# First block's attention: the scores of twelve heads as two rounded products of stacked queries with split keys

## The chip, the core and the metric

The kernel is one program on one NeuronCore of a Trainium2 chip. The core has a matrix engine (TensorE, PE in the profile), a vector engine (VectorE, DVE), a scalar engine (ScalarE, ACT), a general engine (GpSimd, POOL), a queue of transfers (SyncE, SP), an on-chip memory (SBUF) and an accumulation memory of eight banks that PE writes (PSUM, `ps` in the profile). Each engine runs its own instructions in the order in which they were written down and waits for others on semaphores. The metric is the device time of one execution in microseconds (us), as a median over runs. A difference below about 0.3% can't be told from none.

## The reference, cut to what matters

Two transformer blocks run one after the other on 512 tokens. The first block has two layers, and in each of them 16 heads of 64 features attend in three ways. The change touches the products of queries and keys, `s` below, of heads 0 to 7 and of heads 12 to 15.

```python
# heads 0..7: a sliding window of 128 keys, two key heads (bnskd), four query heads on each
s = jnp.einsum('bnqkgd,bnskd->bnkgqs', qb, kb).astype(jnp.float32) * (HEAD_DIM ** -0.5)
...
p = jnp.exp(s - m)
# heads 8..11: blocks of 256 keys (left as they are)
s_own = (jnp.einsum('bhqd,bhsd->bhqs', qc, k_own).astype(jnp.float32) * scale + bias)
...
# heads 12..15: one key head for all, each query keeps its best 128 keys
score = jnp.einsum('bqhs,bqh->bqs', jax.nn.relu(dots), wi)
_, idx = lax.top_k(score, n_keep)
s = jnp.einsum('bqhd,bqkd->bhqk', qc, k_sel).astype(jnp.float32) * scale + bias
p = jax.nn.softmax(s, axis=-1).astype(v.dtype)
```

## The kernel before

Nearly all of the time is matrix products with weights. Each of these is made as three rounded products (`mm3`, lines 228 to 230, type fp32r, high by high, high by low and low by high), for which ACT rounds each weight tile (L192) and DVE subtracts to get what is left (L206). Between two such stages stands the attention of a layer, twice in the first block, from 497 to 597 us of the profile and again a thousand us later.

The attention of a layer is 64 units, numbered u = 16 * query block + head, each of 128 queries and one head, with 128 to 512 keys. Heads 0 to 7 (called A here) see 128 keys in the first query block and 256 in the others. Heads 8 to 11 (B) and 12 to 15 (C) see 128, 256, 384 and 512 keys in the four blocks. The class `Attention` writes the steps of all engines:

- POOL copies the 64 rows of a unit's queries into one of four slots of `q_wide`, whose other 64 rows are zero (`gpsimd`, L1185). It may do so when the unit four before it has been scored. For C units it also adds the chosen keys' mask to the bias (`combine`, L1894).
- PE makes the scores as one product in full fp32 (`score`, L1004; two records for each in the trace) into one of four PSUM banks. It goes through the units in steps: in step u it transposes the probabilities of unit u (L1101), makes the scores of unit u + 3 and then the products with the values of unit u - 1 (L1120). Scores of unit u wait for the queries and for DVE to be done with unit u - 4.
- DVE adds the bias and takes the maximum (`bias`, L1047). At DVE step u that is unit u + 3, in front of which stands, for every third unit, one round of the top-k search (`MAX8` and `MATCH_REPLACE8`, L1830 and L1832), as long as there are rounds left, which is up to unit 52. After each eighth unit come the division by the sum (`normalise`, L1198 to L1208), and twice for each query block the low part of the transposed output (L1233).
- ACT makes the exponentials (L1019) and copies the transposed probabilities (L1164, L1166).

Ahead of this the layer's 18 projection tiles are made. The scores of units 0 to 2 (`first_scores`) stand on PE between tiles 16 and 17, and their biases (`first_biases`) on DVE before the read of tile 17 (L2196).

The second block has a form of the same class in which some units are stacked: the rounded queries fill 64 rows of a slot of `stack` and what the rounding left fills the other 64, the keys stand twice below one another, and two rounded products with the keys' high and low parts (L999, L1000) make the scores. There ACT rounds the queries (L1152), and DVE makes the low half (`low_queries`, L1071), while scores and biases run two units ahead and not three.

The order of the low half and of the bias on DVE is fixed in `vector`:

```python
self.low_queries(dve, u + 3)
self.bias(dve, u + self.ahead, before_unit)   # ahead: 3 in the first block, 2 in the second
```

Of the kernel before, what the change touches and what calls it, by code (L numbers as in the profile page):

```python
# [28 lines left out]
T = 512  # L29
# [24 lines left out]
def program(nc, io):  # L54
# [11 lines left out]
    with top:  # L66
# [827 lines left out]
        class Attention:  # L894
# [10 lines left out]
            def __init__(self, S, tmp, units, groups, turns, q_wide=None, ahead=2, wide_by_act=True, after=None, stack=None):  # L905
                self.stack, self.q_low = stack, S("q_low") if stack is not None else None
# [47 lines left out]
            def counts(self):  # L954

                n, t, sinks = len(self.units), self.t_end[-1], self.sinks_before[-1]
                return {self.q_zero: 0, self.q_ready: n, self.scored: n, self.biased: n,
# [217 lines left out]
            def gpsimd(self, pool, ready, beside):  # L1175

                self.wait(pool, self.q_zero, 1)
                for u, unit in enumerate(self.units):
# [6 lines left out]
                    pool.tensor_copy(self.q_wide[r, u % 4, :], unit["q"]).then_inc(self.q_ready, 1)  # L1185
# [447 lines left out]
        def first_block():  # L1633
            with ExitStack() as ctx:
# [7 lines left out]

                shared = sb(ctx, "shared", [128, 15, T])
# [4 lines left out]
                CKV, KCc = sb(ctx, "ckv", [128, T]), sb(ctx, "kc", [128, T])  # L1648
                VC, QI, KI = sb(ctx, "vc", [128, NQ, 64]), sb(ctx, "q_idx", [128, 2, T]), sb(ctx, "k_idx", [128, T])
# [4 lines left out]
                first_layers(ctx, shared, Hh, Hl, near, far, upc, nsink, tri, QA, KD, VA, QB, KB, VB, QC, CKV, KCc, VC,  # L1654
                             QI, KI, WI, work, best, scratch)

        def first_layers(ctx, shared, Hh, Hl, near, far, upc, nsink, tri, QA, KD, VA, QB, KB, VB, QC, CKV, KCc, VC,
                         QI, KI, WI, work, best, scratch):
# [59 lines left out]
            rows_out = S("rows_out")  # L1718
            line_done, line_mm, const = S("line_done"), S("line_mm"), S("const")
            tables, cond_loaded, cond_done = S("tables"), S("cond_loaded"), S("cond_done")  # L1720
# [48 lines left out]
            ckv_sq, ckv_sum, ckv_root, ckv_inv, ckv_n = S("ckv_sq"), S("ckv_sum"), S("ckv_root"), S("ckv_inv"), S("ckv_n")  # L1769
            kv_mm, kv_out, topk, sel_done, comb_done = S("kv_mm"), S("kv_out"), S("topk"), S("sel"), S("comb")  # L1770
# [7 lines left out]
            for qb in range(NQ):  # L1778
                qs = slice(128 * qb, 128 * qb + 128)
                nk = 128 * (qb + 1)  # L1780
                for h in range(16):
                    r = slice(64 * (h % 2), 64 * (h % 2) + 64)
                    if h < 8:
                        k0 = max(0, qb - 1) * 128
                        units.append({"q": QA[r, h // 2, qs], "init": nsink[:, h:h + 1],
                                      "keys": [(KD[:, h // 4, k0:nk], 0, nk - k0, near[:, h, 256 - (nk - k0):256])],
# [5 lines left out]
                    else:  # L1792
                        bias = far[:, h - 8, 512 - nk:512]
                        if qb:
# [3 lines left out]
                                      "keys": [(KCc[:, 0:nk], 0, nk, bias)],  # L1798
# [8 lines left out]
            for layer in range(DEPTH):  # L1807
                atts.append(Attention(S, at, units, groups, turns, q_wide, 3, wide_by_act=False,
                                      after=atts[0] if layer else None))
# [32 lines left out]
            with nc.Block() as block:  # L1842
# [14 lines left out]
                def pool_layer(pool, layer):  # L1857
# [1209 lines left out]
```

## Time and profile before

| what | value |
|---|---|
| median of 3 runs | 3870.98 us (3861.51 to 3871.17) |
| the profiled execution, its own time | 3870.59 us |
| its span in the profile | 3868.8 us |
| PE busy | 3734.7 us, 97% |
| DVE busy | 2415.1 us, 62% |
| ACT busy | 1377.8 us, 36% |
| mean granted clock of PE | 0.987 |

The span is nearly all of the time, so times read in the trace count as they are. PE is busy nearly everywhere, and a busy PE is no measure of its speed, since a matrix product is counted from its start to its modelled end and the next one starts well before that. So in PE's rows the distance from one start to the next is what counts. The clock is given in parts of 2.4 GHz, and 0.50 is 1.2 GHz.

### The profile page before, as it was taken

Reading aid. Unit: us, or ns where it says so; the run is one execution under the profiler, and the core shown is the slowest. Engines: PE = TensorE matmul, PEld = TensorE weight load, DVE = VectorE, ACT = ScalarE, POOL = GpSimd, SP = SyncE. Lnnn points to the kernel's source line nnn. Section 1 sums busy time; section 2 is a strip of 40 time slices with the busy share of each in tenths; the row PEclk is TensorE's granted clock in tenths of the full one; section 3 lists DMA queues with packets and bytes.
Section 4 is the critical chain, followed back from the end, with each engine's and each line's share of the span. In section 5 each row is a group of like instructions: output and inputs, shape, how many; then the busy total and the mean of one; then the engine's idle time right before and its main releaser. Section 6 shows DMA issues by size and latency. Waiting matters only on the chain. (4 is left out here: it accounts for less than half of the span.)

```text
span 3868.8 us, 51893 instructions
## 1 busy us (share of the span) xinstructions
PE 3734.7 (97%) x18796; PEld 3100.5 (80%) x18796; DVE 2415.1 (62%) x4322; ACT 1377.8 (36%) x2432; POOL 135.1 (3%) x290
## 2 busy tenths in 40 slices
PE   8999999999999999999989899999999889999999
PEld 7888778888888877788878888788888768687887
DVE  6767674767767667476774466455555674646655
ACT  4223354222422244422243466322222354433232
POOL 0000020000000002100000000000000000000000
PEclk9999999999999999999999999999999999999999
DMA  6442303443444321244321110121111110003322
GB/s 246 136 136 93 109 28 112 138 131 120 149 136 139 100 77 44 82 143 135 120 85 54 56 52 20 60 71 60 61 64 60 45 39 1 28 23 98 98 94 75
DMA packets 95881, 340.16 MB, mean 88 GB/s; under 512 B 10799, under 2 KB 13231, under 8 KB 94940
## 3 DMA queue, kind: packets, MB, share of 16 engines
q1 hardware_dynamic: 73728, 264.96, 21.1%
q0 software_dynamic: 17024, 62.97, 4.9%
q10 hardware_dynamic: 4956, 9.90, 0.7%
q8 instruction: 111, 1.82, 0.2%
q14 instruction: 62, 0.51, 0.0%
HBM read 335.64 MB, written 7.39 MB: 89 GB/s over the span
## 5 line engine op out<-in xcount | busy, mean ns | idle before, releaser
L228 PE MATMUL ps<-h_hi,w_hi 128*128 128x512 f32 (+1 forms) x2832 | 1090.5, 385 | 41.5 <-DVE h_lo L506 30.9
L229 PE MATMUL ps<-h_lo,w_hi 128*128 128x512 f32 (+1 forms) x2832 | 1080.3, 381 | 0.0
L230 PE MATMUL ps<-h_hi,w_lo 128*128 128x512 f32 (+1 forms) x2832 | 1079.5, 381 | 0.0
L228 PEld LDWEIGHTS ps<-h_hi,w_hi 128*128 128x128 f32 x2832 | 536.0, 189 | 153.2 <-issue 35.9
L192 ACT ACTIVATE w_hi<-w_first_raw 128x1024 fp32r<-128x1024 f32 x301 | 318.4, 1059 | 933.3 <-PE ps L230 926.6
L229 PEld LDWEIGHTS ps<-h_lo,w_hi 128*128 128x128 f32 x2832 | 535.9, 189 | 102.8 <-issue 3.4
L230 PEld LDWEIGHTS ps<-h_hi,w_lo 128*128 128x128 f32 x2832 | 535.4, 189 | 102.7
L206 DVE TENSOR_TENSOR w_lo<-w_first_raw,w_hi 128x1024 fp32r<-128x1024 f32 x309 | 377.8, 1223 | 339.0 <-ACT w_hi L192 338.6
L228 PE MATMUL ps<-a_hi,w_hi 128*128 128x512 f32 x1472 | 550.5, 374 | 10.0 <-DVE x L790 6.7
L229 PE MATMUL ps<-a_lo,w_hi 128*128 128x512 f32 x1472 | 546.9, 372 | 0.0
L230 PE MATMUL ps<-a_hi,w_lo 128*128 128x512 f32 x1472 | 546.0, 371 | 0.0
L206 DVE TENSOR_TENSOR w_lo<-w_raw,w_hi 128x1024 fp32r<-128x1024 f32 x185 | 226.3, 1223 | 368.6 <-ACT w_hi L192 368.3
L192 ACT ACTIVATE w_hi<-w_raw 128x1024 fp32r<-128x1024 f32 x185 | 195.9, 1059 | 576.7 <-PE ps L230 574.1
L228 PEld LDWEIGHTS ps<-a_hi,w_hi 128*128 128x128 f32 x1472 | 277.0, 188 | 68.1 <-DVE x L790 10.2
L230 PEld LDWEIGHTS ps<-a_hi,w_lo 128*128 128x128 f32 x1472 | 276.8, 188 | 49.3
L229 PEld LDWEIGHTS ps<-a_lo,w_hi 128*128 128x128 f32 x1472 | 277.1, 188 | 47.6
L790 DVE SCALAR_TENSOR_TENSOR x<-ps,x 128x512 f32<-128x512 f32 x352 | 229.2, 683 | 40.6 <-PE ps L230 40.5
L790 DVE SCALAR_TENSOR_TENSOR x<-ps,mod,x 128x512 f32<-128x512 f32 x256 | 188.0, 748 | 90.3 <-PE ps L230 90.2
L1019 ACT ACTIVATE arena<-arena,nm 128x768 f32<-128x768 f32 (+3 forms) x160 | 130.9, 818 | 188.7 <-DVE nm L1047 188.2
L688 ACT ACTIVATE a_hi<-val 128x512 fp32r<-128x512 f32 x88 | 55.6, 632 | 323.2 <-DVE val L760 323.2
L732 DVE TENSOR_TENSOR a_lo<-val,a_hi 128x512 fp32r<-128x512 f32 (+1 forms) x184 | 115.2, 640 | 62.5 <-ACT a_hi L688 33.5
L749 DVE TENSOR_TENSOR mid<-ps,scratch 128x512 f32<-128x512 f32 x88 | 60.5, 687 | 136.5 <-PE ps L230 112.5
(296 smaller groups left out, 4552.8 us busy)
## 6 DMA issues: line engine op xcount, KB each, us to landing
w_first_raw<-in_w_first SPq DMA_DIRECT2D x213, 512.0 KB, 3.5
w_raw<-in_w_first SPq DMA_DIRECT2D x105, 512.0 KB, 3.5
shared<-in_w_ada POOLq DMA_DIRECT2D x96, 512.0 KB, 4.4
w_first_raw<-in_w_mlp SPq DMA_DIRECT2D x64, 512.0 KB, 3.4
w_raw<-in_w_mlp SPq DMA_DIRECT2D x64, 512.0 KB, 3.5
w_first_raw<-in_w_even SPq DMA_DIRECT2D x16, 512.0 KB, 3.6
near_stage<-in_near POOLq DMA_DIRECT2D x32, 256.0 KB, 2.8
w_first_raw<-in_w_odd SPq DMA_DIRECT2D x16, 512.0 KB, 3.4
```

Source lines behind the costliest of these rows:

```text
L192: act.activation(self.hi[:, n % H, :], self.raw(n), ACT.Copy).then_inc(self.hi_done, 1)
L206: dve.tensor_tensor(self.lo[:, n % self.n_hl, :], self.raw(n), self.hi[:, n % self.n_hl, :].bitcast(F32), ALU.subtract).then_inc(self.lo_d ...
L228: pe.matmul(out, lhs[0], rhs[0], start=start, stop=False)
L229: pe.matmul(out, lhs[0], rhs[1], start=False, stop=False)
L230: return pe.matmul(out, lhs[1], rhs[0], start=False, stop=stop)
L688: act.activation(self.hi[0][:, 2 * (c % 2) + j, :], self.val[0][:, j, :], ACT.Copy).then_inc(self.hi_done, 1)
L732: m = dve.tensor_tensor(self.lo[s][:, a, :], self.val[s][:, j, :], self.hi[s][:, a, :].bitcast(F32), ALU.subtract)
L749: dve.tensor_tensor(mid, bank, inv, ALU.mult).then_inc(self.gate_done, 1)
L790: m = dve.scalar_tensor_tensor(out=stream["x"][:, o, :], in0=ps[:, self.down_bank(8 * c + o, s), 0:stream["n"]], scalar=self.gains(s, o), ...
L1019: act.activation(self.row(u, 0, n), self.row(u, 0, n), ACT.Exp, bias=tmp["nm"][:, u % 16:u % 16 + 1], scale=-1.0, accum_out=tmp["sums"][:, ...
```

## The change

The 48 A and C units of each layer become stacked units, as in the second block. POOL writes the rounded queries into `stack` and not into `q_wide`; DVE gets a new instruction for each of these units, the low half of the queries (64 x 128); PE makes their scores as two rounded products and not as one in fp32. The keys are split once in each layer: ACT rounds KD (128 x 1024) and KC (128 x 512, in place of the plain copy), DVE subtracts for the low parts. The B units stay as they are. `stack` and the low part of KC lie where other tensors lay, so POOL's first copy now waits for the latent's products (`kv_mm`). Some semaphores are merged; by this PE's first matmul waits for one more small transfer, `cond`.

```diff
 # the class Attention, gpsimd
-                    pool.tensor_copy(self.q_wide[r, u % 4, :], unit["q"]).then_inc(self.q_ready, 1)
+                    wide = self.stack if "stack" in unit else self.q_wide
+                    pool.tensor_copy(wide[r, u % 4, :], unit["q"]).then_inc(self.q_ready, 1)
 # units of heads 0 to 7
-                                      "keys": [(KD[:, h // 4, k0:nk], 0, nk - k0, near[:, h, 256 - (nk - k0):256])],
+                                      "stack": True,
+                                      "keys": [((KDh[:, h // 4, k0:nk], KDl[:, h // 4, k0:nk]), 0, nk - k0, near[:, h, 256 - (nk - k0):256])],
 # units of heads 12 to 15
-                                      "keys": [(KCc[:, 0:nk], 0, nk, bias)],
+                                      "stack": True, "keys": [((KCh[:, 0:nk], KCl[:, 0:nk]), 0, nk, bias)],
 # POOL, before its first copy
+                        if u == 0:
+                            eng.wait_ge(kv_mm, 2 * layer + 2)
 # PE
-                        pe.wait_ge(tables, 32)
+                        pe.wait_ge(tables, 48)
 # ACT, beside projection tiles 9 and 11
+                        if j == CKV_AFTER + 1:
+                            act.wait_ge(evac, layer * N_EVAC + 5)
+                            act.activation(KDh[:, :, :], KD, ACT.Copy).then_inc(k_split, 1)
-                            act.activation(KCc[:, :], ps[:, 7, :], ACT.Copy).then_inc(kv_out, 1)
+                            act.activation(KCh[:, :], ps[:, 7, :], ACT.Copy).then_inc(k_split, 1)
 # DVE, ahead of the first biases, at tile 17
                         if j == N_IN1 - 1:
+                            for u in range(3):
+                                att.low_queries(dve, u)
                             att.first_biases(dve, combined)
 # DVE, beside projection tiles 10 and 12
+                        if j == CKV_AFTER + 2:
+                            dve.wait_ge(k_split, 2 * layer + 1)
+                            dve.tensor_tensor(KDl[:, :, :], KD, KDh[:, :, :].bitcast(F32), ALU.subtract
+                                              ).then_inc(kv_out, 1)
+                        if j == CKV_AFTER + 4:
+                            dve.wait_ge(k_split, 2 * layer + 2)
+                            dve.tensor_tensor(KCl[:, :], ps[:, 7, :], KCh[:, :].bitcast(F32), ALU.subtract
+                                              ).then_inc(kv_out, 1)
```

The scores and the low half are the second block's code, which was there before:

```python
def low_queries(self, dve, u):
    if u >= len(self.units) or "stack" not in self.units[u]:
        return
    a = 64 * (u % 2)
    self.wait(dve, self.q_ready, u + 1)
    dve.tensor_tensor(self.stack[64 - a:128 - a, u % 4, :], self.units[u]["q"],
                      self.stack[a:a + 64, u % 4, :].bitcast(F32), ALU.subtract).then_inc(self.q_low, 1)
...
if "stack" in self.units[u]:     # in score, on PE
    self.wait(pe, self.q_low, self.stacked[u + 1])
```

Three places show how the instructions stand. First DVE in the middle of the attention, at A units 20 to 22 of 256 keys, before the change (L1047 is the bias and its second row the read of the maximum, L1233 the low part of a transposed output):

```order
L1047 ISA scratch,nm<-ps,bias_a,minus_sinks 128x256 [waits turned_195,scored_191]
L1047 ISA nm 128x1
L1047 ISA scratch,nm<-ps,bias_a,minus_sinks 128x256 [waits turned_195,scored_191]
L1047 ISA nm 128x1
L1233 TENSOR_TENSOR h_lo<-ps,h_hi 128x128 [waits ot_hi_205]
L1233 TENSOR_TENSOR h_lo<-ps,h_hi 128x128 x3
L1830 MAX best_47<-topk 128x8 [waits topk_185]
L1832 MATCH_REPLACE topk<-best_47,topk 128x512 [waits topk_185]
L1047 ISA deep_scores,nm<-ps,bias_a,minus_sinks 128x256 [waits turned_195,scored_191]
```

and the same place after it:

```order
L1047 ISA scratch,nm<-ps,bias_a,minus_sinks 128x256 [waits turned_201,scored_197]
L1047 ISA nm 128x1
L1071 TENSOR_TENSOR stack<-shared,stack 64x128 [waits q_ready_196]
L1047 ISA scratch,nm<-ps,bias_a,minus_sinks 128x256 [waits turned_201,scored_197]
L1047 ISA nm 128x1
L1234 TENSOR_TENSOR h_lo<-ps,h_hi 128x128 [waits ot_hi_211]
L1234 TENSOR_TENSOR h_lo<-ps,h_hi 128x128 x3
L1071 TENSOR_TENSOR stack<-shared,stack 64x128 [waits q_ready_196]
L1841 MAX best_53<-topk 128x8 [waits topk_190]
L1843 MATCH_REPLACE topk<-best_53,topk 128x512 [waits topk_190]
L1047 ISA deep_scores,nm<-ps,bias_a,minus_sinks 128x256 [waits turned_201,scored_197]
```

The low half of a unit's queries (L1071) stands right in front of that unit's bias and behind the bias of the unit before it.

Second, PE at A units of 256 keys, one step before the change (transposes, scores, values):

```order
L1101 MATMUL ps<-ident,deep_scores 128x128 [waits pt_dve_197,exped_194]
L1101 MATMUL ps<-ident,deep_scores 128x128
L1004 MATMUL ps<-shared,q_wide 128x256 [waits biased_192,q_ready_190]
L1120 MATMUL ps<-shared,scratch 128x64 [waits pt_dve_197,pt_act_196]
L1120 MATMUL ps<-shared,scratch 128x64
```

and after it:

```order
L1101 MATMUL ps<-ident,deep_scores 128x128 [waits pt_dve_203,exped_200]
L1101 MATMUL ps<-ident,deep_scores 128x128
L999 MATMUL ps<-kd_hi,stack 128x256 [waits biased_198,q_low_194,q_ready_196]
L1000 MATMUL ps<-kd_lo,stack 128x256
L1120 MATMUL ps<-shared,scratch 128x64 [waits pt_dve_203,pt_act_202]
L1120 MATMUL ps<-shared,scratch 128x64
```

The scores' first product has got a wait on `q_low`, which DVE counts up in L1071.

Third, DVE at the start of the attention, before the change (L2196 is the read of projection tile 16, L206 the split of a weight tile):

```order
L2196 SCALAR_TENSOR_TENSOR shared<-ps,scratch 128x512 [waits w_used_63]
L206 TENSOR_TENSOR w_lo<-w_first_raw,w_hi 128x1024 [waits w_hi_done_61]
L1047 ISA scratch,nm<-ps,bias_a,minus_sinks 128x128 [waits scored_191,biases_in_73,nsink_188]
L1047 ISA nm 128x1
L1830 MAX best_47<-topk 128x8 [waits topk_185]
```

and after it (L2214 is the same read):

```order
L2214 SCALAR_TENSOR_TENSOR shared<-ps,scratch 128x512 [waits w_used_69]
L206 TENSOR_TENSOR w_lo<-w_first_raw,w_hi 128x1024 [waits w_hi_done_67]
L1071 TENSOR_TENSOR stack<-shared,stack 64x128 [waits q_ready_196] x3
L1047 ISA scratch,nm<-ps,bias_a,minus_sinks 128x128 [waits scored_197,biases_in_79,nsink_193]
L1047 ISA nm 128x1
```

The bias stood right behind L206, and now three low halves stand between. PE's first scores, which stand behind tile 16 there and here, now wait for an instruction that DVE begins after L206.

## Rows read from the trace of the kernel before

**Rows 1.** The page: busy time by engine, and a weight transfer's landing time, last number.

```profile
PE 3734.7 (97%) x18796; PEld 3100.5 (80%) x18796; DVE 2415.1 (62%) x4322; ACT 1377.8 (36%) x2432; POOL 135.1 (3%) x290
...
w_first_raw<-in_w_first SPq DMA_DIRECT2D x213, 512.0 KB, 3.5
```

**Rows 2.** Stretches of layer 1's attention: length, busy time by engine, PE clock, transfers.

```profile
503.00:518.00 15.00, 10.87 (x66) 9.85 (x65) 12.98 (x48) 9.12 (x41) 3.83 (x13) 0.77 0.10 37
518.00:549.00 31.00, 27.70 (x199) 24.32 (x198) 25.23 (x92) 22.13 (x90) 9.84 (x28) 1.00 0.00 1
549.00:575.00 26.00, 23.80 (x160) 20.39 (x159) 18.72 (x65) 17.02 (x58) 8.90 (x20) 0.95 0.01 2
```

**Rows 3.** PE's waits from 480 to 640 us: sum, times, longest.

```profile
PE ps L1120 <- ACT scratch L1164: 5.6, 7, 1.5
```

**Rows 4.** Timeline of PE, one fp32 unit of 256 keys: start, duration, instruction.

```profile
540.52 0.39 PE L1101 MATMUL ps<-ident,deep_scores 128*128 128x128 f32 x2
540.75 0.60 PE L1004 MATMUL ps<-shared,q_wide 128*128 128x256 f32 x2
541.18 0.55 PE L1120 MATMUL ps<-vc,scratch 128*128 128x64 f32 x4
541.57 0.39 PE L1101 MATMUL ps<-ident,scratch 128*128 128x128 f32 x2
```

**Rows 5.** Timeline of PE, one stacked unit of 256 keys in the second block.

```profile
2367.43 0.39 PE L1101 MATMUL ps<-ident,arena 128*128 128x128 f32 x2
2367.58 0.36 PE L999 MATMUL ps<-ka_hi,stack 128*128 128x256 f32 x1
2367.78 0.28 PE L1000 MATMUL ps<-ka_lo,stack 128*128 128x256 f32 x1
2367.90 1.45 PE L1120 MATMUL ps<-vb,arena 128*128 128x64 f32 x12
```

**Rows 6.** Timeline of DVE there: bias after scores, then bias and low half.

```profile
2368.10 0.48 DVE L1047 CUSTOM_DVE_ANT_0 arena<-ps,zeros,minus_sinks 128x256 f32<-128x256 f32 x1 [0.41 <-PE ps L1000]
...
2370.81 0.48 DVE L1047 CUSTOM_DVE_ANT_0 arena<-ps,zeros,minus_sinks 128x256 f32<-128x256 f32 x1
...
2371.33 0.29 DVE L1071 TENSOR_TENSOR stack<-qa,stack 64x128 fp32r<-64x128 f32 x1
```

**Rows 7.** Timeline of the projection's end and the attention's start, all engines.

```profile
475.05 0.69 DVE L2196 SCALAR_TENSOR_TENSOR shared<-ps,scratch 128x512 f32<-128x512 f32 x1 [2.48 <-PE ps L230]
...
496.62 0.83 PE L1004 MATMUL ps<-shared,q_wide 128*128 128x128 f32 x6
...
497.97 1.23 DVE L206 TENSOR_TENSOR w_lo<-w_first_raw,w_hi 128x1024 fp32r<-128x1024 f32 x1 [0.46 <-ACT w_hi L192]
...
499.12 0.35 DVE L1047 CUSTOM_DVE_ANT_0 scratch<-ps,bias_a,minus_sinks 128x128 f32<-128x128 f32 x1
...
504.12 1.23 DVE L206 TENSOR_TENSOR w_lo<-w_raw,w_hi 128x1024 fp32r<-128x1024 f32 x1 [0.46 <-ACT w_hi L192]
...
505.27 0.34 DVE L1047 CUSTOM_DVE_ANT_0 deep_scores<-ps,bias_a,minus_sinks 128x128 f32<-128x128 f32 x1
```

**Rows 8.** Timeline of DVE: a top-k round, a division by the sum, a low part.

```profile
529.91 0.69 DVE L1830 MAX8 best<-topk 128x8 f32<-128x512 f32 x1
...
531.31 0.41 DVE L1047 CUSTOM_DVE_ANT_0 scratch<-ps,bias_bc 128x256 f32<-128x256 f32 x1
...
532.52 0.42 DVE L1047 CUSTOM_DVE_ANT_0 deep_scores<-ps,bias_bc 128x256 f32<-128x256 f32 x1 [0.45 <-PE ps L1004]
...
534.11 0.68 DVE L1830 MAX8 best<-topk 128x8 f32<-128x512 f32 x1
...
570.94 0.88 DVE L1233 TENSOR_TENSOR h_lo<-ps,h_hi 128x128 fp32r<-128x128 f32 x4 [0.93 <-ACT h_hi L1172]
```

**Rows 9.** Groups of L1047 and of POOL's copies: shortest, median, longest ns, first and last start.

```profile
L1047 DVE CUSTOM_DVE_ANT_0 deep_scores<-ps,scratch x6: 415/552/691, 536.8 to 589.3; 128x256 f32<-128x256 f32 x2, 128x384 f32<-128x384 f32 x2, 128x512 f32<-128x512 f32 x2
...
L1185 POOL COPY q_wide<-shared x128: 279/288/1365, 468.6 to 1567.5; 64x128 f32<-64x128 f32 x128
```

**Rows 10.** Stretches around idle time of PE, then a stacked unit at half clock.

```profile
504.00:506.00 2.00, 0.78 (x5) 0.58 (x5) 1.88 (x4) 0.60 (x4) 0.38 (x2) 1.00 0.00 0
...
508.00:510.00 2.00, 1.84 (x9) 1.85 (x10) 1.76 (x6) 1.39 (x8) 0.29 (x1) 0.50 0.11 45
...
2197.12 0.56 PE L999 MATMUL ps<-ka_hi,stack 128*128 128x256 f32 x1
2197.48 0.41 PE L1000 MATMUL ps<-ka_lo,stack 128*128 128x256 f32 x1
```

More of the change, by code:

```diff
@@ L905, in __init__ @@
             def __init__(self, S, tmp, units, groups, turns, q_wide=None, ahead=2, wide_by_act=True, after=None, stack=None):
-                self.stack, self.q_low = stack, S("q_low") if stack is not None else None
+                self.stack, self.q_low = stack, None if stack is None else after.q_low if after else S("q_low")
                 self.stacked = [sum("stack" in unit for unit in units[:k]) for k in range(len(units) + 1)]
@@ L1641, in first_block @@
                 tri = sb(ctx, "causal", [128, 128])
+                with ExitStack() as place:
+                    sb(place, "before_kd", [128, 12, T])
+                    KDl = sb(place, "kd_lo", [128, 2, T], F32R)
                 shared = sb(ctx, "shared", [128, 15, T])
@@ L1647, in first_block @@
                 KD, VA = shared[:, 12:14, :], shared[:, 14, :].rearrange("p (q n) -> p q n", n=128)
-                CKV, KCc = sb(ctx, "ckv", [128, T]), sb(ctx, "kc", [128, T])
-                VC, QI, KI = sb(ctx, "vc", [128, NQ, 64]), sb(ctx, "q_idx", [128, 2, T]), sb(ctx, "k_idx", [128, T])
+                with ExitStack() as place:
+                    stack, KCl = sb(place, "stack", [128, 4, 128], F32R), sb(place, "kc_lo", [128, T], F32R)
+                CKV = sb(ctx, "ckv", [128, T])
+                sb(ctx, "place_of_kc_lo", [128, T])
+                VC = sb(ctx, "vc", [128, NQ, 64])
+                with ExitStack() as place:
+                    KDh, KCh = sb(place, "kd_hi", [128, 2, T], F32R), sb(place, "kc_hi", [128, T], F32R)
+                QI, KI = sb(ctx, "q_idx", [128, 2, T]), sb(ctx, "k_idx", [128, T])
                 WI = sb(ctx, "w_idx", [128, NQ, 4])
@@ L1653, in first_block, with first_layers @@
                 scratch = sb(ctx, "scratch", [128, 8, 512])
[L1654 to L1658, printed above, removed]
+                first_layers(ctx, shared, Hh, Hl, near, far, upc, nsink, tri, QA, KD, VA, QB, KB, VB, QC, CKV, VC,
+                             KDh, KDl, KCh, KCl, stack, QI, KI, WI, work, best, scratch)
+        def first_layers(ctx, shared, Hh, Hl, near, far, upc, nsink, tri, QA, KD, VA, QB, KB, VB, QC, CKV, VC,
+                         KDh, KDl, KCh, KCl, stack, QI, KI, WI, work, best, scratch):
             S = Sems()
@@ L1808, in first_layers @@
                 atts.append(Attention(S, at, units, groups, turns, q_wide, 3, wide_by_act=False,
-                                      after=atts[0] if layer else None))
+                                      after=atts[0] if layer else None, stack=stack))
             TOPK = (NQ - 1) * 2 * TOPK_ROUNDS
@@ L1999, in pe_layer @@
                         if j == N_IN1 - 2:
-                            pe.wait_ge(kv_out, 2 * layer + 2)
+                            pe.wait_ge(kv_out, 3 * layer + 3)
                         if j == N_IN1 - 1:
@@ L2017, in ready @@
                         eng.wait_ge(evac_v, NQ * layer + NQ)
-                        eng.wait_ge(kv_out, 2 * layer + 2)
+                        eng.wait_ge(kv_out, 3 * layer + 3)
                         eng.wait_ge(relu_done, 12 * layer + 12)
@@ L2048, in act_layer @@
                     if layer == 0:
-                        act.wait_ge(cond_loaded, 16)
+                        act.wait_ge(tables, 48)
                         act.activation(raw_cond, raw_cond, ACT.Silu).then_inc(cond_done, 1)
```

12 lines of the change are left out of this document (6 added, 6 removed).

## The prediction, made before the changed kernel was run

> **What bounds the kernel now.** I read the page first, then a table of stretches over the attention of layer 1, then PE's waits in it, and last the instructions one by one. The page shows PE busy for 97% of the span [rows 1]; outside the attention nothing is changed but a few instructions. Inside it PE is busy 10.9 of 15, 27.7 of 31 and 23.8 of 26 us, DVE 13.0, 25.2 and 18.7, and the clock is 0.77, 1.00 and 0.95 [rows 2]. PE's longest sum of waits is 5.6 us, for ACT [rows 3], and ACT waits for DVE's biases. So PE leads, and DVE, which also has the top-k rounds, is close behind. What keeps them apart is slack: scores run three units ahead of the transposes and may be four ahead of the biases. An A unit of 256 keys takes PE 1.05 us: 0.23 from the transposes to the scores, 0.43 for the scores, 0.39 for the values [rows 4]. From the bias of unit 3 at 505.27 [rows 7] to that of unit 63 at 589.3 [rows 9] it is 84.0 us for 60 units, 1.40 us each.
>
> **What PE is spared.** A stacked unit of the second block takes 0.47 us from transposes to values (2367.43 to 2367.90) [rows 5], an fp32 one 0.66 (540.52 to 541.18) [rows 4]. That is 0.19 less for 256 keys, and with the same slope 0.3 for 384 and 0.4 for 512. A layer has 28, 4 and 4 such units: 5.3 + 1.2 + 1.6 = 8.1 us, 16 us for two layers. For the 12 units of 128 keys no rounded product of that width is in the trace. At the slope of [rows 5] two of them take 0.37 us, more than half of what 256 keys take; their own cost lies between that and two fp32 products of 128 keys (0.22 each), and I take the first. The rows show the two products at 0.48 us in all where the fp32 one is paced at 0.43, so it is the shorter run-up and overlap that gain, not the sum of their durations. The Trainium skill says ("FP8 and Floating Point Precision", "TensorE Precision Notes") that true fp32 is four passes through the array; two rounded products by that rule would be half of the score's 0.43, which gives 10 us a layer instead of 8.
>
> **What the change locks.** This is the step that decides. PE's scores of unit v now wait for the low half of v. On DVE that instruction stands behind the bias of unit v - 1 (the first order listing of the change), and that bias waits for the scores of v - 1. So scores, bias, low half and next scores follow one another with nothing beside them that could shorten the way. The Trainium skill says of VectorE's queue ("TensorE: Matmul & The Clock Gate", "Architectural detail: the array is 16× 32×32, not 1× 128×128") that it is strictly first in, first out; no row shows DVE overtaking either. The second block has the same code and no such lock, since there the bias runs two units ahead and the low half three.
>
> The length of the lock for an A unit of 256 keys: bias start to low half start 0.52 (2370.81 to 2371.33), low half 0.29 [rows 6], hand-over to PE 0.08 (an estimate, above the 0.04 from the end of 2367.78's product to 2368.10), start 0.03, the two products 0.20 + 0.28 = 0.48 [rows 5], back to DVE 0.04 [rows 6]: 1.44 us, against 1.05 today. In the 0.89 us in which DVE has the word PE does its 0.62 of values and transposes and then idles. For other widths the bias changes as in [rows 9] (0.415, 0.552, 0.691; A is 0.065 longer than C by 0.48 against 0.415, and 0.14 shorter for 128 keys by 0.34 in [rows 7]) and the products by 0.11 for each 128 keys. That gives A128 1.19, C128 1.12, C256 1.37, C384 1.62, and for C512 1.87, where PE's own work (0.45 transposes, 0.70, 0.78 values) is 1.95.
>
> Sum over units 4 to 63 of one layer: 4 A128 4.8; 3 C128 3.4; 24 A256 34.6; C of the other blocks 3 x 1.37 + 3 x 1.62 + 3 x 1.95 = 14.8; together 57.6. The four stretches of B and the first C unit behind it (bias to bias): PE may run ahead over B at 0.55, 1.05, 1.27 and 1.48 a unit (rows 4's steps with 0.22 for each 128 keys of scores); DVE needs 2.45, 4.1, 5.8 and 3.6 us with its rounds and low parts, so 2.45, 4.2, 5.8 and 6.2 stand. Behind come the division (bias to next instruction 1.59, 532.52 to 534.11 [rows 8]), a low half and a locked score (0.8 to 1.15): 4.8 + 6.7 + 8.6 + 9.2 = 29.3. **Top-k rounds**: a round is 1.40 us (529.91 to 531.31) [rows 8] and now lies between low half and bias, where 0.63 us (0.52 for 128 keys) of it is covered by the scores. Three at 128 keys (0.9 each), ten at 256 or 384 (0.76), and the last round's extra 0.4: 10.8. Today they are taken up by the slack. **Divisions** within A units add 0.87 three times and **low parts** 0.95 three times [rows 8]: 5.5. The sum is 103.2 us against 84.0: +19.2 a layer.
>
> **The start.** Today the first scores run at 496.62, and the bias of unit 0 stands at 499.12 behind the weight split of 497.97 [rows 7]. The first low half can begin only there, so PE idles from 496.6 to 499.6, and tile 17 comes 3.3 us later. After it the low half of unit 3 again stands behind a weight split (504.12, then ending 508.6), then 0.29 + 0.11 + 0.40 us, and the bias of unit 3 starts at 509.4, not 505.27: +4.1 a layer.
>
> **The clock.** After PE had been busy 0.78 of 2 us the clock went to 0.50 [rows 10]. In the lock PE has 1.1 us of work in 1.44, and about 0.55 in 1.2 to 2 in the first query block. A locked unit at 1.2 GHz needs 2 x 0.62 on PE's own and 0.77 for the products (2197.12 to the end of 2197.48's [rows 10]): 2.0, 0.6 more. From none to all of some 37 units this is 0 to 22 us a layer; I take 5, eight units, since today's 0.77, 1.00 and 0.95 [rows 2] show the clock coming back after such spells.
>
> **The rest, taken as nothing.** DVE's splits of the keys are one subtraction as long as L206 (1.2) and one half as wide (0.7), ACT's rounding of KD 1.1. DVE idles 2.48 us before one read of a tile and 0.46 before each weight split [rows 7], and the tiles are split three ahead; without this cover they cost at most 3 us a layer. POOL's copy is 0.29 [rows 9]; it becomes a rounding one and has four units' time. Queued behind it are the masks of the C units, which wait for biases as before. POOL's first copy, at 468.6 today [rows 9], waits about 1 us longer, 28 us ahead of its use at 496.6 [rows 7]. PE's first product waits for one more small transfer: 0, at most the 3.5 of a large one [rows 1].
>
> The sum: the profiled execution took 3870.6 us, as the median (3871.0). 2 x (19.2 + 4.1) = 46.6 and 2 x 5 for the clock: 3927 us, 1.5% slower.
>
> **Rivals.** (1) The lock holds PE at half clock for most of the attention: 2 x (23.3 + 18) gives 3953, at the end 2 x (23.3 + 22) gives 3961. For it speaks the clock of 0.77 at 503 to 518 [rows 2], against it that PE at half clock is busy all the time and then has got its clock back each time. (2) PE's saving comes through: DVE works ahead and the low halves are always there in time. Then 3871 - 16 = 3855, or 3851 by the rule of four passes. It holds if the lock is shorter than PE's own unit (0.86); the rows add up to 1.44, so it needs the order on DVE to be other than listed. (3) Nothing measurable: today's mean of 1.40 us a unit has in it the same rounds and divisions, and if they overlapped with the lock as they do now, the lock of 1.44 would hardly show: 2 x 4 us for the start and 0 to 4 for the rest, 3879 to 3883. Against it: between low half and bias a round can't overlap with anything of the lock but the scores. (4) The change doesn't do what it says, if the 128-key products are slow: +0.2 on 15 units, 6 us for both layers, a part of the range.
>
> **How the numbers follow.** Forecast, the lock with the clock near today's or somewhat lower (3897 to 3945): 0.75. Rival 1, above 3945: 0.15. Rival 3: 0.05. Rival 2: 0.05. The time is the forecast's, 3927. Its lower end takes no clock cost and locks 15% shorter on 2 x 58 us, 3897 to 3900; the upper end goes to most of rival 1, 3960. Left out are rivals 2 and 3 and the far ends. A measurement of this kernel tells about 0.3% (12 us) from no change: faster 0.05, within 0.04, slower 0.91.
>
> **What would show it.** In the changed kernel's trace: PE's L999 must wait for L1071 in almost every stacked unit, with distances of 1.4 to 1.5 us at 256 keys and 2.2 where a round stands; PE idle of about 3 us ahead of the first scores; the bias of unit 3 to that of unit 63 near 103 us and something for the clock, not 84; products of a stacked unit 0.48 us. It would be wrong if PE's waits on L1071 were few, or if the stretches after the attention gave time back, for which I see no way since PE is busy all through them.

## The result, and the profile after

The changed kernel took 3932.67 us as a median (3930.08 to 3935.89) against 3870.98 (3861.51 to 3876.27) for the kernel before, five runs of each: the ratio is 1.0166, with a 95% interval from 1.0154 to 1.0177. Forecast were 3927 us and a range of 3897 to 3960. The profiled execution has a span of 3930.9 us against 3868.8, so 62.1 us have to be found.

The page of the changed kernel, which answers to [rows 1]:

```profile
PE 3757.7 (96%) x18796; PEld 3117.1 (79%) x18796; DVE 2450.6 (62%) x4422; ACT 1383.1 (35%) x2434; POOL 133.6 (3%) x290
```

PE's busy time grew by 23 us though its products got shorter; DVE has 100 more records and 35 us more. Where the time went shows in one stretch, from the bias of unit 3 to that of unit 63 of layer 1. First the kernel before, then the changed one (length, then busy time of PE, weight loads, DVE, ACT and POOL, PE's clock, transfers):

```profile
505.27:589.28 84.01, 75.27 (x495) 63.88 (x495) 61.62 (x221) 56.39 (x208) 28.09 (x67) 0.94 0.02 8
```

```profile
510.96:621.35 110.39, 87.22 (x503) 73.28 (x502) 76.36 (x263) 57.84 (x208) 28.71 (x69) 0.78 0.02 6
```

The loop takes 110.4 and not 84.0 us, and the same in layer 2 (84.0 and 110.5): 52.9 of the 62.1 us. PE has 23 us without work in it, 9 before, and a clock of 0.78, not 0.94. No engine is full: 110 us with DVE at 76 and PE at 87 is what a chain across two engines looks like. The chain itself, first PE and then DVE (start, duration, instruction, in brackets the idle time before):

```profile
541.77 0.39 PE L1101 MATMUL ps<-ident,deep_scores 128*128 128x128 f32 x2
543.09 0.36 PE L999 MATMUL ps<-kd_hi,stack 128*128 128x256 f32 x1 [0.93 <-issue]
543.29 0.28 PE L1000 MATMUL ps<-kd_lo,stack 128*128 128x256 f32 x1
543.40 0.55 PE L1120 MATMUL ps<-shared,scratch 128*128 128x64 f32 x4
```

```profile
542.70 0.29 DVE L1071 TENSOR_TENSOR stack<-shared,stack 64x128 fp32r<-64x128 f32 x1
...
544.42 0.48 DVE L1047 CUSTOM_DVE_ANT_0 deep_scores<-ps,bias_a,minus_sinks 128x256 f32<-128x256 f32 x1
...
544.94 0.29 DVE L1071 TENSOR_TENSOR stack<-shared,stack 64x128 fp32r<-64x128 f32 x1
545.84 0.48 DVE L1047 CUSTOM_DVE_ANT_0 deep_scores<-ps,bias_a,minus_sinks 128x256 f32<-128x256 f32 x1 [0.62 <-PE ps L1000]
```

The low half of 542.70 ends at 542.99, and L999 starts at 543.09, after PE had waited 0.93 us since its transposes. The next bias is 1.42 us behind the last (544.42 to 545.84), with no round between them. Two A units of 256 keys at half clock read:

```profile
532.43 0.48 DVE L1047 CUSTOM_DVE_ANT_0 scratch<-ps,bias_a,minus_sinks 128x256 f32<-128x256 f32 x1 [0.91 <-PE ps L1000]
...
534.14 0.48 DVE L1047 CUSTOM_DVE_ANT_0 deep_scores<-ps,bias_a,minus_sinks 128x256 f32<-128x256 f32 x1 [0.90 <-PE ps L1000]
```

That is 1.71. PE's waits from 480 to 640 us, in [rows 3] 5.6 us for ACT, are now these:

```profile
PE ps L999 <- issue: 19.8, 27, 1.6
...
PE ps L999 <- DVE stack L1071: 5.6, 2, 2.9
...
PE ps L999 <- POOL stack L1186: 1.9, 3, 0.8
```

The profile names DVE for only two of the 32, and POOL's copy into the same slot for three. For the other 27 it says "issue", which is time in which it sees no releaser. By the word alone one would miss the cause. In the timeline each of the 32 ends 0.10 us behind the end of a low half, the two that name DVE 0.15 us. The other 16 of the layer's 48 stacked units show no such wait or one of at most 0.12 us; among them are the last three of 512 keys, where PE's own work is the longer.

The start, which answers to [rows 7]:

```profile
497.78 1.23 DVE L206 TENSOR_TENSOR w_lo<-w_first_raw,w_hi 128x1024 fp32r<-128x1024 f32 x1 [0.46 <-ACT w_hi L192]
499.04 0.92 DVE L1071 TENSOR_TENSOR stack<-shared,stack 64x128 fp32r<-64x128 f32 x3
...
507.68 0.69 DVE L2214 SCALAR_TENSOR_TENSOR shared<-ps,scratch 128x512 f32<-128x512 f32 x1 [5.60 <-PE ps L230]
...
510.96 0.35 DVE L1047 CUSTOM_DVE_ANT_0 deep_scores<-ps,bias_a,minus_sinks 128x128 f32<-128x128 f32 x1 [0.60 <-PE ps L1000]
```

```profile
499.47 0.30 PE L999 MATMUL ps<-kd_hi,stack 128*128 128x128 f32 x1 [2.88 <-DVE stack L1071]
499.60 0.27 PE L1000 MATMUL ps<-kd_lo,stack 128*128 128x128 f32 x1
```

PE waits 2.88 us for the first low half, which stands behind a weight split, and the bias of unit 3 comes at 510.96 and not at 505.27.

### The profile page after: what moved, and what is told of

Same layout as the page of the kernel before. It is cut to its first block and busy times, and to the rows that moved or that the text cites. A ratio compares the mean times of both kernels' runs of the same rounds, so it can differ in the third digit from the quotient of the medians.

```text
span 3930.9 us, 52001 instructions
## 1 busy us (share of the span) xinstructions
PE 3757.7 (96%) x18796; PEld 3117.1 (79%) x18796; DVE 2450.6 (62%) x4422; ACT 1383.1 (35%) x2434; POOL 133.6 (3%) x290
## 5 line engine op out<-in xcount | busy, mean ns | idle before, releaser
L206 DVE TENSOR_TENSOR w_lo<-w_first_raw,w_hi 128x1024 fp32r<-128x1024 f32 x309 | 378.1, 1224 | 338.1 <-ACT w_hi L192 337.5
L206 DVE TENSOR_TENSOR w_lo<-w_raw,w_hi 128x1024 fp32r<-128x1024 f32 x185 | 226.4, 1224 | 369.4 <-ACT w_hi L192 369.1
L749 DVE TENSOR_TENSOR mid<-ps,scratch 128x512 f32<-128x512 f32 x88 | 60.6, 688 | 136.5 <-PE ps L230 112.4
```

What stands on the lines that cost most here:

```text
L206: dve.tensor_tensor(self.lo[:, n % self.n_hl, :], self.raw(n), self.hi[:, n % self.n_hl, :].bitcast(F32), ALU.subtract).then_inc(self.lo_d ...
L749: dve.tensor_tensor(mid, bank, inv, ALU.mult).then_inc(self.gate_done, 1)
```

## Experiments

All ran as whole kernels beside the kernel before, and times are medians; loop and clock are those of one profiled execution each. "Loop" is bias 3 to bias 63 in layers 1 and 2. The theory: the low half's place in DVE's queue locks PE to DVE. The rivals: the rounded products, POOL's rounding copy or the key splits cost the time; DVE's extra work does; the start does.

| kernel | us | loop | clock in loop 1 |
|---|---|---|---|
| before | 3871 | 84.0, 84.0 | 0.94 |
| changed | 3932.7 | 110.4, 110.5 | 0.78 |
| low half one step earlier (e1) | 3884.6 | 93.1, 90.8 | 0.85 |
| the same, start as it was (e2) | 3894.7 | 91.7, 91.0 | 0.87 |
| start alone (e3) | 3928.2 | 112.4, 113.0 | 0.74 |
| no low half (e4) | 3858.6 | 79.2, 77.5 | 0.94 |
| low half on POOL (e5) | 3857.2 | 79.1, 79.3 | 0.96 |
| low half twice (e6) | 3983.1 | 132.7, 132.9 | 0.68 |
| lock with an fp32 product (e7) | 3944.3 | 117.0, 118.9 | 0.84 |
| transposes twice (e8) | 3936.4 | 111.5, 110.1 | 0.85 |
| round ahead of the low half (e9) | 3976.7 | 130.8, 127.8 | 0.65 |
| low half two steps earlier (e10) | 3889.3 | 92.5, 92.3 | 0.83 |
| e1 with the low half twice (e11) | 3922.2 | 107.0, 107.5 | 0.76 |

**The order, mended.** `low_ahead` is 4 in the first block and 3 in the second.

```diff
-                    self.low_queries(dve, u + 3)
+                    self.low_queries(dve, u + self.low_ahead)
-                        if j == N_IN1 - 1:
-                            for u in range(3):
+                        if j == N_IN1 - 2:
+                            for u in range(4):
                                 att.low_queries(dve, u)
+                        if j == N_IN1 - 1:
                             att.first_biases(dve, combined)
```

> The changed kernel with one thing moved: in the first block DVE makes the low half of unit v one step earlier, behind the bias of v - 2 and not of v - 1, and those of units 0 to 3 ahead of the read of projection tile 16. Same work, same products. Theory (the order on DVE locks PE): the lock is gone, PE's 8 us a layer come through in part, and DVE, which was busy 25.2 of 31 us and gets 0.33 us more for each of 48 units, becomes the slower of the two in places: about 3866, range 3855 to 3875. Rival (the rounded products, POOL's rounding copy or the key splits cost the time): 3925 to 3935 as before. Rival (half of each, the clock stays low): 3890 to 3910.

Measured: 3884.55 (3882.06 to 3889.88), ratio to before 1.004, interval 1.0027 to 1.0054. Making the low halves earlier, by one place in the loop and ahead of the read of tile 16 at the start, gave 48 of the 62 us back, which the rounded products, copy and splits, all still there, can't have cost. But it is slower than forecast, and slower than the kernel before. In its busiest stretch DVE is the engine that is nearly full (26.8 of 30 us, in the third column of busy times):

```profile
550.00:580.00 30.00, 24.55 (x173) 21.28 (x173) 26.83 (x85) 18.25 (x63) 9.69 (x23) 0.94 0.00 1
```

**Loop and start apart.** In e2 the early low halves stand where the changed kernel has its three, behind the weight split; in e3 only the start is moved.

```diff
 # e2, with low_ahead 4
                         if j == N_IN1 - 1:
-                            for u in range(3):
+                            for u in range(4):
                                 att.low_queries(dve, u)
 # e3, with u + 3 in the loop
+                        if j == N_IN1 - 2:
+                            for u in range(3):
+                                att.low_queries(dve, u)
                         if j == N_IN1 - 1:
-                            for u in range(3):
-                                att.low_queries(dve, u)
                             att.first_biases(dve, combined)
```

> As the run with the earlier low halves, but those of units 0 to 3 stand where the changed kernel has those of 0 to 2, ahead of the first biases. Theory: the wait of the first scores (3 us) and tile 17 behind it stay, so it is slower than the run with both by the start's share: bias of unit 3 came 5.7 us later than before in each layer, less the 1.2 us or so that unit 3's own low half no longer adds: 9 us in all, about 3875. Rival (nothing is lost at the start, since the slack of the units takes it up): as the run with both.

> The changed kernel with the low halves of units 0 to 2 alone made earlier, ahead of the read of projection tile 16; in the loop the order stays. Theory: the lock in the loop stays with its cost, and the start gives back 2 x (4 to 5.7) us: 3921 to 3925. Rival (the start is the main cost): below 3900.

Measured: 3894.67 and 3928.18 (3926.19 to 3934.06). The start costs 10 us with the loop mended (3894.7 against 3884.6) and 4.5 with the loop as it is; expected were 9 and 8 to 11 (e2's 3875 missed by 20 us because e1's forecast, to which it added the 9, missed by 19). Each ratio's interval reaches 5 to 6 us to either side, so the 10 is clear of noise and the 4.5 isn't. The loop is the main cost, the start a small one. With the start mended alone the loop got 2 us a layer longer, and its clock fell from 0.78 to 0.74. In layer 1 all of that lies in units whose clock wasn't that of the changed kernel; unit 39 alone took 2.45 us at half clock and not 1.42 at full.

**The same low half on another engine.**

```diff
 # gpsimd, behind the copy; DVE makes none in the first block
+                    self.low_queries(pool, u, True)
+                    if 'stack' in unit:
+                        self.wait(pool, self.q_low, self.stacked[u + 1])
```

> The changed kernel with the low half made by POOL, right behind its copy, and no longer by DVE. Theory: the lock through DVE is gone and DVE has no more work than before the change, so PE's saving of 8 us a layer comes through if POOL keeps pace. POOL's subtraction isn't in a trace; its addition of 128 x 256 took 0.73 and of 128 x 384 1.00 us, at that slope 128 columns take 0.45 (an estimate), with the copy 0.29 and a hop 0.85 a unit, below the 1.3 of PE. For C units the mask adds 0.73 to 1.27: 1.6 to 2.1 against 1.3 to 1.9, some waits. About 3858, range 3852 to 3880. Rival (POOL's part or the rounded products are the cost): above 3925.

Measured: 3857.2 (3853.38 to 3866.28, 9 runs), ratio 0.997, interval 0.9961 to 0.998: 0.3% faster than the kernel before, and 1.9% faster than the changed one. The stretch of the loop and the group of POOL's low halves:

```profile
510.20:589.29 79.09, 67.44 (x495) 59.46 (x495) 61.88 (x220) 54.88 (x208) 46.11 (x108) 0.96 0.03 8
```

```profile
L1071 POOL TENSOR_TENSOR stack<-shared,stack 64x128 fp32r<-64x128 f32 x44 | 19.9, 453 | 3.6
```

POOL takes 0.45 us for what DVE does in 0.29, and it doesn't matter, since POOL had the time.

**No low half at all.** The subtraction and PE's wait for it are left out and the other rows of a slot are zero. The stack is now the zeroed `q_wide`, as a rounded type, and B's queries are rounded in it as well.

```diff
 # in score and low_queries
-                if "stack" in self.units[u]:
+                if "stack" in self.units[u] and self.q_wide is not self.stack:
                     self.wait(pe, self.q_low, self.stacked[u + 1])
-                if u >= len(self.units) or "stack" not in self.units[u]:
+                if u >= len(self.units) or "stack" not in self.units[u] or self.q_wide is self.stack:
                     return
```

> The changed kernel without the low half of the queries: no such instruction on any engine and no wait for it, the other 64 rows of a slot are zero, and the scores are the rounded queries times the keys' two parts. This leaves out what the rounding of the queries leaves. Two rounded products as in the changed kernel, the key splits and POOL's rounding copy stay. Theory (the products, the splits and the copy cost nothing, the low half's place was all of the loss): as fast as the run in which POOL made the low half or a little faster, 3853 to 3858. Rival (the low half on POOL costs something of its own): 3848 or less.

Measured: 3858.55 (3853.89 to 3860.96), ratio 0.9972. Its time is that of the run with POOL's low half, so that one is free within the noise. What the two rounded products give is 4.9 and 4.8 us a layer in e5's loops (84.0 to 79.1 and 79.3) and 4.8 and 6.6 here (to 79.2 and 77.5), not the 8.1 of the prediction.

**The low half twice, locked and unlocked.**

```diff
+                for k in range(2):
+                    if k:
+                        self.wait(dve, self.q_low, self.stacked[u + 1] - 1)
                     dve.tensor_tensor(self.stack[64 - a:128 - a, u % 4, :], self.units[u]["q"],
                                       self.stack[a:a + 64, u % 4, :].bitcast(F32), ALU.subtract).then_inc(self.q_low, 1)
```

> The changed kernel with each low half of the first block made twice, the second after a wait for the first, and PE waiting for the second. Theory: the low half stands on the locked path in every stacked unit, 0.29 and some 0.06 for the wait, for 48 units a layer less the few C512 units that are PE's: 2 x 46 x 0.35 = 32 us more, 3965; 27 to 36 more. Rival (DVE has slack and the loss is elsewhere): 3933 as the changed kernel.

Measured: 3983.06 (3981.05 to 3986.58), 50 us more and not 32. A pair takes 0.60:

```profile
573.40 0.47 DVE L1047 CUSTOM_DVE_ANT_0 deep_scores<-ps,bias_a,minus_sinks 128x256 f32<-128x256 f32 x1
...
573.91 0.61 DVE L1074 TENSOR_TENSOR stack<-shared,stack 64x128 fp32r<-64x128 f32 x2
575.43 0.48 DVE L1047 CUSTOM_DVE_ANT_0 deep_scores<-ps,bias_a,minus_sinks 128x256 f32<-128x256 f32 x1 [0.90 <-PE ps L1000]
```

The unit is 2.03, at half clock, against 1.71: the second instruction shows in full, so the direction is the theory's. 0.31 x 46 is 14.3 a layer; the loops grew by 22.3 and 22.4. The clock fell from 0.78 to 0.68, which is 36 us more at 1.2 GHz. A unit of 1.71 loses 0.29 there, or 0.17 us for each us, and the run with doubled transposes below gives 0.10. So this is 4 to 6 us. The rest is in the units whose mask POOL adds. There a pair reads:

```profile
596.19 1.29 DVE L1074 TENSOR_TENSOR stack<-shared,stack 64x128 fp32r<-64x128 f32 x2
```

Six of the second low halves in each layer take 0.70 to 1.29 us and not 0.29, each beside a mask addition of POOL (the last section shows this in e1). That is 4.1 us a layer more, and with it all of the 22 are found.

> The run with the low halves one step earlier, with each low half made twice, the second after a wait for the first. Theory (with the order mended DVE's load sets the time): nearly the whole second instruction shows, 0.31 (0.60 for a pair against 0.29 in the changed kernel with doubled low halves) x 46 x 2 = 29 us more, 3913, range 3903 to 3918. Rival (DVE has slack there and PE's own work or the clock sets the time): 3885 to 3895.

Measured: 3922.17 (3919.25 to 3925.85), 38 us more than e1 by the medians; the loop grew by 13.9 and 16.7 us and the profiled spans by 31 (3888.1 to 3918.9). With the order mended nearly the whole added instruction still shows, which is DVE's load setting the time: DVE's busy time in layer 1's loop rose from 79.0 to 95.4 us. The next run says the same from the other side; it is e1 with `low_ahead` 5 and the low half of unit 4 made ahead of the loop.

> As the run in which DVE made the low halves one step earlier (3884.6), but two steps earlier: behind the bias of v - 3. Same work. That run's loop from bias 3 to bias 63 took 93.1 and 90.8 us a layer against 84.0 before the change and 79.1 with POOL making the low half. Theory (what is left there is DVE's own load, 0.29 and gaps for each of 48 units on an engine that was busy 0.89 of the time): no change, 3881 to 3888. Rival (part of the lock is still in that order): the loop falls towards 84 or less, 3860 to 3875.

Measured: 3889.34 (3885.17 to 3891.41), ratio 1.0054, at the upper end of what was expected. One more step of slack gives nothing (loop 92.5 and 92.3), so what is left of the loss in e1 isn't order.

**The lock with the old product.** DVE's instruction and PE's wait stay, POOL copies without rounding, and PE makes one fp32 product with the keys' high part, which leaves out their low part.

```diff
-                        pe.matmul(self.scores_ps(u, col, col + n), self.stack[:, u % 4, :], k_hi, start=True, stop=False)
-                        m = pe.matmul(self.scores_ps(u, col, col + n), self.stack[:, u % 4, :], k_lo, start=False, stop=True)
+                        pe.matmul(self.scores_ps(u, col, col + n), q, k_hi.bitcast(F32), start=True, stop=True).then_inc(self.scored, 1)
```

> The changed kernel with the A and C scores made again as one fp32 product from q_wide (on the keys' high part, which leaves out their low part), but with DVE's instruction and PE's wait for it kept: POOL copies without rounding, DVE subtracts the copy from the queries into the zero half, and the result is zero. Theory (the lock costs, the products don't): the lock is longer by the fp32 product's own length, 0.60 from first start to last end (0.22 and 0.39) against 0.48, so 2 x 40 x 0.12 = 10 us more than the changed kernel, 3942, range 3936 to 3950. Rival (the rounded products or POOL's rounding cost time): below 3915.

Measured: 3944.3 (3943.04 to 3945.17), forecast 3942. It is slower still, as an fp32 product of 0.60 in the lock asks for, and with nothing rounded in the queries. This clears the rounded products and POOL's rounding.

**The round in front of the low half.** `before_unit` here makes the round alone; its waits stay with the bias.

```diff
+                    before_unit(dve, u + 3, "rounds")
                     self.low_queries(dve, u + 3)
```

> The changed kernel with the top-k round of every third unit in front of the low half and not between low half and bias. Same work. The prediction took 0.63 us of a round's 1.40 as covered by the scores (0.52 at 128 keys), because the low half is out before the round; in the changed kernel's trace a unit with a round took 2.05 bias to bias at 1.2 GHz where one without took 1.71, so much of the round was covered. Theory (scores follow the low half and nothing else): in front of the low half the round is covered by nothing, 13 locked rounds x 0.55 to 0.63 x 2 layers = 14 to 16 us more, 3948, range 3943 to 3955. Rival (rounds are taken up elsewhere, their place is nothing): 3933.

Measured: 3976.68 (3972.51 to 3978.41), 44 us more and not 15. A unit with a round, then one without:

```profile
529.24 0.29 DVE L1047 CUSTOM_DVE_ANT_0 scratch<-ps,bias_bc 128x128 f32<-128x128 f32 x1 [0.80 <-PE ps L1000]
...
532.06 0.29 DVE L1047 CUSTOM_DVE_ANT_0 scratch<-ps,bias_bc 128x128 f32<-128x128 f32 x1 [0.80 <-PE ps L1000]
...
533.47 0.29 DVE L1047 CUSTOM_DVE_ANT_0 deep_scores<-ps,bias_bc 128x128 f32<-128x128 f32 x1 [0.80 <-PE ps L1000]
```

2.82 against 1.41: the round's 1.41 is now covered by nothing, as the theory has it. In the changed kernel a unit of 256 keys with a round took 2.25 at half clock and one without 1.71, so there 0.86 of the round was covered, not the 0.63 that I had taken at full clock. Added up unit by unit, the 13 locked units with a round are 10.0 and 10.5 us longer in the two layers, of the 20.4 and 17.2 by which the loops grew. Of the rest 8.2 and 5.7 us are in units that ran at a lower clock than in the changed kernel: units 23, 39 and 53 took 2.45 and not 1.42 in both layers. The medians' 44 is 6 more than both layers' loops. By the profiles 3.1 us of it lie ahead of the first bias (503.10 against 500.05) and 3.1 behind the last bias of layer 2's loop, where nothing was changed; among the profiled executions the first bias comes anywhere from 497.2 to 505.3 us.

**More work for PE in the lock.** The transposes of each stacked unit are made twice.

```diff
-                        for j in range(nb):
+                        for j in [*range(nb)] * (2 if "stack" in self.units[u] and self.banks == 4 else 1):
```

> The changed kernel with the transposes of each stacked unit's probabilities made twice into the same place, so that PE has 0.2 us more of work in a unit of 256 keys, in the time in which it waits for DVE; the lock's path is not touched. In the changed kernel the granted clock was 0.50 in about 10 of the 4 us stretches of layer 1's attention and each locked unit of 256 keys took 1.71 instead of 1.42 there. Theory (the clock falls because PE idles in the lock, and costs 7 to 9 us a layer): the clock comes back in part, and the kernel is up to 12 us faster, 3921 to 3930. Rival (the clock costs next to nothing or is not set by the idle time): 3933, or up to 8 slower where the second transposes don't fit at 1.2 GHz.

Measured: 3936.37 (3931.94 to 3944.78). The clock of the whole loop rose from 0.78 to 0.85, but the time didn't fall. Unit by unit there are two effects. From the bias of unit 30 to that of unit 39 the work on DVE is the same, and PE was at full clock in one kernel and not in the other. First this kernel, then the changed one:

```profile
563.36:580.20 16.84, 12.56 (x100) 11.31 (x99) 12.55 (x43) 8.74 (x34) 2.61 (x9) 0.96 0.01 1
```

```profile
556.82:575.13 18.31, 16.37 (x82) 14.36 (x81) 12.65 (x43) 9.21 (x33) 2.60 (x9) 0.58 0.00 0
```

The clock is worth 1.47 us here. 0.58 is 15.4 us of 18.31 at 1.2 GHz and 0.96 is 1.3 of 16.84, which makes 0.10 us for each. It is a mean of unlike prices. In the changed kernel a unit with a round took 2.25 at half clock (unit 19) and 2.24 at full (unit 49), so there the clock cost nothing; one without took 1.71 against 1.42; and unit 39, in which PE also transposes four outputs, took 2.45 in e3 against 1.42. Elsewhere the second transposes stand on PE's own path, as at unit 21 (2.88 us, 2.45 before) and in the B units 57 to 59 (1.69 each, 1.47 to 1.70 before), and take this back. So with less idle time on PE the clock came back in part: the idle time does bring it down. By these prices that costs some us a layer, not most of the loss; the median of this run, with a spread of 13 us, doesn't show a gain.

## Why the prediction was right, step by step

**The lock** was the step that decided, and it held. Unit of 256 keys: forecast 1.44, measured 1.42. C of 512 keys: forecast 1.95 as PE's own work, measured 1.95 (units 61 to 63). With a round: forecast 0.76 more, 2.20; measured 2.24 (unit 49). e1 and e5 show that most of the loss is the place of the instruction and not the work beside it. One sign fell short: L999 was to wait for L1071 in almost every stacked unit, and it did in 32 of 48.

**The loop** was put at 103.2 us plus 5 for the clock, 108.2; it was 110.4. The prediction took 8 units at 0.6 for the clock. In the trace the clock of 0.78 is 49 us at 1.2 GHz, some 28 units of 1.71, at 0.10 to 0.17 us for each us 5 to 8 us. So 0 to 3 of the 2.2 us are the clock, and which other term was short isn't shown. (The parts of the sum as written give 0.3 or so less than 103.2: the last stretch of B adds up to 8.9 and not 9.2.) That 5 came near is luck, since both factors were off, in opposite directions. The price was too high, since PE's unit at half clock was put at 1.24 + 0.77 = 2.0. It is 1.72:

```profile
560.40 0.95 PE L1120 MATMUL ps<-vc,scratch 128*128 128x64 f32 x4
561.14 0.63 PE L1101 MATMUL ps<-ident,deep_scores 128*128 128x128 f32 x2
561.56 0.55 PE L999 MATMUL ps<-kd_hi,stack 128*128 128x256 f32 x1
561.91 0.42 PE L1000 MATMUL ps<-kd_lo,stack 128*128 128x256 f32 x1
562.12 0.52 PE L1120 MATMUL ps<-vc,scratch 128*128 128x64 f32 x2
```

From start to start that is 0.74, 0.42, 0.35 and 0.21: I had counted the products to their end (0.77), where the next unit's values start after 0.56. PE has no idle time there, and some units later the clock is back (1.00 in units 39 to 53). The number was too low, since I took today's clock as a guide for a loop in which PE idles in each unit. Rival 1 (most of the attention at half clock) was nearer on the share, which is nearly half of the loop, and wrong on the price.

**The start** was put at 4.1 us; bias 3 came 5.7 us later. PE's wait was forecast from 496.6 to 499.6, and the first product ran at 499.47. Most of the missing 1.6 us is tile 17, which was forecast 3.3 us later and came 4.7 us later (its read at 507.68, not 502.98): its products were paced at half clock from 501 to 504 us after that wait, a cost that the prediction left out. Together 2 x (26.4 + 5.7) is 64.2, 2 more than the spans differ by; so some of it comes back behind the loop.

**What PE is spared** was in the sum only for the locked units' own path. As a gain it was put at 8.1 us a layer in the rival of 3855. With the lock away (e5) it was 3857, which looks like that rival's number and isn't its sum: the loops give 4.9 and 4.8 us a layer, and the ratio's interval leaves 8 to 15 us for the whole. PE's products are as short as said, and its wait for ACT, 5.6 in [rows 3], is 8.3 there:

```profile
PE ps L1120 <- ACT scratch L1164: 8.3, 9, 1.9
```

ACT waits for DVE's biases. I read this as DVE, with its rounds, taking the rest; no run took the rounds out to show it.

**128 keys** (rival 4): a pair of rounded products is paced at 0.13 + 0.19, and its own time to the end is 0.40, where the prediction had 0.37 and, at the start, 0.40; no penalty shows. **The rest at nothing**: e4 and e5 carry the key splits, POOL's rounding copy and the one more small transfer, and are faster than before, so these are within the few us that were allowed. **Rival 3**, today's slack taking the lock in, fell by its own argument: the loop grew by 26 us a layer.

**What the prediction didn't ask** is what happens once the order is mended. I had expected 3866 and measured 3884.6. The low half is new work on an engine that already sets part of the pace. In e1's loops it took 15.3 us a layer, 43 instructions of which six stood beside POOL's mask additions and took 3.0 us more than 0.29 each; the loops are 14.0 and 11.5 us longer than e5's, a loss that has nothing to do with order. By the ratios the loss splits so: 1.0166 to 1.004 for the order, loop, start and clock together, 49 us; 1.004 to 0.997 for DVE's load, with what the clock adds (0.85 against 0.96 in layer 1), 27 us; less the 12 us that PE gains (0.997 to 1).

## What to carry to other kernels

When a producer for one engine is queued behind a consumer of that same engine's last result, the two engines take turns, and no engine looks full: add up one turn of the chain and compare it with each engine's own work, and shift the producer one unit forward or to a third engine. Count as well whether the engine that gets the new instruction has room for it, since an instruction that was taken for nothing cost 12 to 14 us a layer here even in the right place. And PE's idle time in such a loop may lower its clock and be paid for again in part: the forecasts of e6 and e9, which left this out, came out 18 and 29 us short, in e6 by 8 us for VectorE's waits behind GpSimd as well.

## What the hardware showed beside this

In e1, where DVE's low halves are free to fall anywhere, six in each layer's loop took longer than 0.29 us, 0.39 to 1.31 (line numbers are one higher there). First DVE, then POOL:

```profile
542.55 0.75 DVE L1072 TENSOR_TENSOR stack<-shared,stack 64x128 fp32r<-64x128 f32 x1
...
567.82 1.12 DVE L1072 TENSOR_TENSOR stack<-shared,stack 64x128 fp32r<-64x128 f32 x1
```

```profile
542.44 0.72 POOL L1906 TENSOR_TENSOR scratch<-bias_bc,topk 128x256 f32<-128x256 f32 x1
...
567.78 1.00 POOL L1906 TENSOR_TENSOR scratch<-bias_bc,topk 128x384 f32<-128x384 f32 x1
```

All six began while a mask addition of POOL was under way and ended 0.15 us after it (543.30 after 543.16, 568.94 after 568.78). A low half that begins first keeps its 0.29 us: in the changed kernel all six that stand beside an addition in a layer begin 0.1 to 0.2 us ahead of it, as at 554.07 with the addition at 554.17. DVE's biases, which read one operand from PSUM, run beside such additions in their usual time, as in the kernel before:

```profile
551.25 1.00 POOL L1894 TENSOR_TENSOR scratch<-bias_bc,topk 128x384 f32<-128x384 f32 x1
...
551.59 0.55 DVE L1047 CUSTOM_DVE_ANT_0 scratch<-ps,bias_bc 128x384 f32<-128x384 f32 x1
```

The Trainium skill says ("SBUF — State Buffer", "SBUF: two separate sides") that a VectorE operation with two inputs in SBUF and a GpSimd one that reads SBUF exclude each other for a whole instruction, whichever begins first. The trace agrees, with 0.75 and 1.12 for 0.29 where POOL began first, and 0.29 where DVE did.
